# Six changes of order and of engine in a fused two-block fp32 transformer kernel on one core

## The reference

```python
def first_block(x, mem, ...):
    hn = rmsnorm(h, norm_mix_g)
    h = h + hybrid_mixer(hn, w_in, ...)          # gMLP, conformer conv, mLSTM, then @ w_out
    hn = rmsnorm(h, norm_x_g); mn = rmsnorm(mem, norm_mem_g)
    h = h + cross_attention(hn, mn, w_xq, w_xkv, w_xo)   # 4 heads of 256, 256 memory rows
    hn = rmsnorm(h, norm_ffn_g)
    h = h + conv_glu(hn, w_up, conv_f_w, conv_f_b, w_down)   # d_ff 2816
    return rmsnorm(h, final_g)

def second_block(x, mem, ...):
    z = rms_norm(h, g_mix_pre) @ w_in
    ya = swa_with_sinks(...)     # local attention, 8 heads of 64, window of 3 chunks of 64
    yh = hgrn2(...)              # gated linear recurrence
    y = concat([ya, yh]) @ w_out; h = h + rms_norm(y, g_mix_post)
    h = h + rms_norm(cross_attention_2(...), g_x_post)
    h = h + rms_norm((silu(u @ w_gate) * (u @ w_up)) @ w_down, g_ffn_post)
```

## Time and profile before

| | us |
|---|---|
| median of 3 runs | 2730.49 (2730.25 to 2730.56) |
| the profiled execution, its own time | 2729.75 |
| span of the profile | 2727.4 |
| PE busy | 2683.9 (98%) |
| DVE busy | 1768.8 (65%) |
| ACT busy | 1114.4 (41%) |
| POOL busy | 1307.8 (48%) |

### The profile page before, as it was taken

The page is one execution under the profiler, slowest core; times in us unless marked ns, Lnnn a source line. Parts: engine busy times, 40 slices in busy tenths (PEclk is TensorE's granted clock), DMA queues, the critical chain, the costliest instruction groups (busy, mean ns, idle before and its releaser), DMA issues.

```text
span 2727.4 us, 35252 instructions
## 1 busy us (share of the span) xinstructions
PE 2683.9 (98%) x12722; PEld 2196.3 (81%) x12722; DVE 1768.8 (65%) x2101; ACT 1114.4 (41%) x1854; POOL 1307.8 (48%) x766
## 2 busy tenths in 40 slices
PE   8999999999999999999999999999999999999999
PEld 6888787878778888888887778778887888888886
DVE  7888643345966666976845456784548655557775
ACT  4256622132433333444423524562446333334444
POOL 4313213545699999100466331454154888884002
PEclk9999999999999999999999999999999999999999
DMA  4101224342122222650422110332022433347413
GB/s 155 39 25 39 101 90 152 121 177 101 51 89 73 88 79 83 223 190 28 163 93 96 52 39 24 116 121 73 22 79 81 171 134 138 120 150 270 166 59 139
DMA packets 108712, 287.02 MB, mean 105 GB/s; under 512 B 9904, under 2 KB 20400, under 8 KB 107824
## 3 DMA queue, kind: packets, MB, share of 16 engines
q1 hardware_dynamic: 98336, 252.55, 26.4%
q10 hardware_dynamic: 10256, 32.86, 3.3%
HBM read 226.12 MB, written 59.24 MB: 105 GB/s over the span
## 4 chain that ended last, share of the span: by engine, by line
PE 89%; DVE 5%; ACT 2%; POOL 2%; issue 2%; DMA 0%; ACTq 0%; DVEq 0%; POOLq 0%; SPq 0%
PE products L993 22%; PE others L1515 14%; PE products L1515 13%; PE products L1088 8%; PE others L1598 7%; PE products L1598 7%; PE products L1426 2%; PE others L993 1%; PE products L1010 1%; PE products L1401 1%; PE others L1401 1%; PE products L1117 1%; PE products L1773 1%; PE others L1706 1%; PE others L1088 1%
## 5 line engine op out<-in xcount | busy, mean ns | idle before, releaser
L993 PE MATMUL products<-act_hi,w_hi 128*128 128x512 f32 x864 | 347.0, 402 | 1.4 <-DVE act_lo L2853 1.3
L993 PE MATMUL products<-act_hi,w_lo 128*128 128x512 f32 x864 | 336.9, 390 | 0.0
L993 PE MATMUL products<-act_lo,w_hi 128*128 128x512 f32 x864 | 336.9, 390 | 0.0
L871 POOL TENSOR_TENSOR w_lo<-w_raw,w_hi 128x512 fp32r<-128x512 f32 x200 | 309.7, 1557 | 37.6 <-ACT w_hi L2342 37.6
L786 POOL TENSOR_TENSOR w_hi<-w_raw,small 128x1024 fp32r<-128x1024 f32 x53 | 105.6, 1993 | 449.5 <-PE products L993 226.6
L993 PEld LDWEIGHTS products<-act_hi,w_hi 128*128 128x128 f32 x864 | 162.2, 188 | 41.7 <-issue 7.3
L2342 ACT ACTIVATE w_hi<-w_raw 128x512 fp32r<-128x512 f32 x240 | 146.2, 626 | 113.1 <-PE others L1515 50.1
L993 PEld LDWEIGHTS products<-act_hi,w_lo 128*128 128x128 f32 x864 | 162.2, 188 | 34.9
L993 PEld LDWEIGHTS products<-act_lo,w_hi 128*128 128x128 f32 x864 | 162.5, 188 | 30.8 <-issue 0.2
L904 POOL TENSOR_TENSOR w_lo<-w_raw,w_hi 128x512 fp32r<-128x512 f32 x8 | 10.4, 1294 | 363.7 <-ACT w_hi L2382 363.7
L793 POOL TENSOR_TENSOR w_lo<-w_raw,w_hi 128x512 fp32r<-128x512 f32 x64 | 99.2, 1571 | 136.5 <-ACT w_hi L2696 136.5
(11 more groups left out here) (638 smaller groups left out, 7377.7 us busy)
## 6 DMA issues: line engine op xcount, KB each, us to landing
w_raw<-wstream SPq DMA_DIRECT2D x147, 512.0 KB, 3.5
w_raw<-wstream SPq DMA_DIRECT2D x168, 256.0 KB, 2.6
work<-wstream SPq DMA_DIRECT2D x52, 512.0 KB, 4.4
parked_sums<-work SPq DMA_DIRECT2D x20, 1024.0 KB, 4.8
parked_hidden<-work SPq DMA_DIRECT2D x40, 512.0 KB, 2.9
raw<-parked_sums SPq DMA_DIRECT2D x28, 512.0 KB, 7.8
raw<-parked_hidden SPq DMA_DIRECT2D x20, 512.0 KB, 6.8
work<-parked_hidden SPq DMA_DIRECT2D x20, 512.0 KB, 7.7
```

Of the source, the lines that this page charges most:

```text
L871: pool.tensor_tensor(ring_lo[slot], part_source[(n - 1) % 7], ring_hi[slot].bitcast(F32), ALU.subtract)\
L993: last = pe.matmul(out[:, c], a[:, ws, w], x[:, k, c], start=(k == 0 and i == 0), stop=(k == KT - 1 and i == 2))
```

## The change

It moves and reassigns work; the arithmetic is the same up to which engine does it. (1) Block 19's high part is made by ACT and its low part by DVE, and ordered in the counts of y1_hi and y1_lo at position 7; POOL only counts it. The convolution's mean sums of tile 1 stand at part 5 instead of 4; the logs are spread between the head copies. (2) In the loop behind out1 DVE's key copy comes first, then the low weight part, then the sum and the low part of h; sums of the last tile are moved into the loop. (3) `weight_sums(3)` and `(4)` wait for chunks of the probabilities, and sums 7, 8, 9 stand behind splits q0+10, q0+11 and q0+12. (4) The root for ffn1 is made behind the third difference (k = 2). (5) Two squares are summed together in ffn2a. (6) In z2 PV of unit n - 5 stands right before the scores of n - 3 at k = 2, in the tiles n = 5 to 18; tile 19 does both of the last units.

```diff
+THIRD_AT = 7
@@ split_third, POOL
-                if b == 19:
-                    pool.wait_ge(s("product_quarters"), 4 * 17)
...
-            split_third(19, (s("y1_lo"), 8))
+            pool.wait_ge(s("y1_lo"), THIRD_AT + 1)
+            pool.sem_inc(s("weights_split"), 1)
+            made_elsewhere[0] += 1
@@ weight_sums, POOL
+                probs = {3: (3, 4), 4: (7, None)}.get(n, (None, None))
                 pool.wait_ge(s("block_moved"), 32 * (n + 1))
+                if probs[0]:
+                    pool.wait_ge(s("xa_probs"), XA0["1"] + probs[0])
                 pool.tensor_tensor(low_(1), low_(0), low_(1), ALU.add).then_inc(s("parts_summed"), 1)
                 pool.tensor_tensor(low_(0), up_(0), low_(0), ALU.subtract).then_inc(s("parts_summed"), 1)
+                if probs[1]:
+                    pool.wait_ge(s("xa_probs"), XA0["1"] + probs[1])
...
-                for n in {2: (0,), 4: (1,), 6: (2,), 9: range(3, 8), 10: (8,), 12: (9,)}.get(b - q0, ()):
+                for n in {2: (0,), 4: (1,), 6: (2,), 9: range(3, 7), 10: (7,), 11: (8,), 12: (9,)}.get(b - q0, ()):
@@ out1, PE
                     if i == 4:
                         last_back()
+                    if i == 5:
                         pe.wait_ge(s("ml_out"), NCH)
                         convolved_sums(1, "std_mean", lambda c: W[:, 3, c], s("cb_done"), 2)
...
-                    pe.wait_ge(s("y1_lo"), i + 1)
+                    pe.wait_ge(s("y1_lo"), i + 1 + (i >= THIRD_AT))
@@ ffn2a, PE
+                def squares_behind(k):
+
+                    if k and k % 2 == 0:
+                        square_of(k - 2)
+                        square_of(k - 1)
...
-                                  (lambda k: square_of(k - 1) if k else None) if (half, j) == (1, 0) else None)
+                                  squares_behind if (half, j) == (1, 0) else None)
                         if (half, j) == (1, 0):
-                            square_of(KT - 1)
+                            squares_behind(KT)
@@ z2, PE
+                        if k == 2 and n >= 5:
+                            window_values(n - 5)
                         if k == 2 and n < 19:
                             window_scores(n - 3)
                         if k == 4 and 4 <= n < 20:
                             window_turn(n - 4)
-                        if k == 6 and 4 <= n < 20:
+                        if k == 6 and n == 19:
                             window_values(n - 4)
@@ out1, ACT
+            def third_weight_high():
+
+                act.wait_ge(s("weights_loaded1"), 16 * 10)
+                act.wait_ge(s("product_quarters"), 4 * 17)
+                act.activation(w3_hi[:, 0, :], w_raw[:, 1, :], ACT.Copy).then_inc(s("y1_hi"), 1)
...
             head_high(6)
+            third_weight_high()
             convolved_squares(1)
             head_high(7)
+            convolved_logs(0)
             head_high(8)
+            convolved_logs(1)
+            head_high(9)
             convolved_roots()
-            head_high(9)
@@ ffn1, ACT
-            differences_high("ffn1")
-            roots("ffn1")
+            differences_high("ffn1", lambda k: roots("ffn1") if k == 2 else None)
@@ z2, ACT
+                if n > 4:
+                    window_out(n - 5)
                 turned_probs(n - 4)
                 if n < 19:
                     window_exponentials(n - 3)
-                window_out(n - 4)
+            window_out(15)
@@ out1, DVE
+            def third_weight_low():
+
+                dve.wait_ge(s("y1_hi"), THIRD_AT + 1)
+                dve.tensor_tensor(w3_lo[:, 0, :], w_raw[:, 1, :], w3_hi[:, 0, :].bitcast(F32), ALU.subtract).then_inc(s("y1_lo"), 1)
...
                 head_y(i)
+                if i == THIRD_AT:
+                    third_weight_low()
                 y1_low(i)
@@ behind out1, DVE
             for n in range(2, 2 * KT + 2):
-                if n < KT:
-                    weights_low("1", n)
-                if 2 <= n < 5:
+                if n < KT + 2:
+                    key("1", n - 2)
+                weights_low("1", n)
+                if n < 4:
+                    sums("q1", KT - 4 + n)
+                if n < 5:
                     split_low("q1", n - 2, h_tile, "x1")
-                if 2 <= n < KT + 2:
-                    key("1", n - 2)
-                if n >= KT:
-                    weights_low("1", n)
```

More of the change, by code:

```diff
@@ L2164, in convolved_squares, with convolved_logs @@
                 act.activation(W[:, n, :], W[:, 2 + n, :], ACT.Square, scale=0.125).then_inc(s("std_sq"), 1)
-            def convolved_roots():
[L2168 to L2172, removed]
+            def third_weight_high():
+                act.wait_ge(s("weights_loaded1"), 16 * 10)
+                act.wait_ge(s("product_quarters"), 4 * 17)
+                act.activation(w3_hi[:, 0, :], w_raw[:, 1, :], ACT.Copy).then_inc(s("y1_hi"), 1)
+            def convolved_logs(n):
+                act.wait_ge(s("std_var"), n + 1)
+                for h in range(2):
+                    last = act.activation(W[:, n, h * HALF:(h + 1) * HALF], std_slots[n][h], ACT.Ln, bias=epsc[:, 1:2])
+                last.then_inc(s("std_root"), 1)
+            def convolved_roots():
                 act.wait_ge(s("std_root"), 2)
@@ L2222, in _ @@
                 y1_high(10 + n)
-            act.wait_ge(s("y1_lo"), len(Y1_PARTS))
+            act.wait_ge(s("y1_lo"), len(Y1_PARTS) + 1)
             def memory(x):
@@ L3055, in y1_low @@
             def y1_low(i):
-                dve.wait_ge(s("y1_hi"), i + 1)
+                dve.wait_ge(s("y1_hi"), i + 1 + (i >= THIRD_AT))
                 dve.tensor_tensor(act_lo[:, Y1_PARTS[i][0], y1_tokens(i)], y1_source(i), hi_as_f32[:, Y1_PARTS[i][0], y1_tokens(i)],
                                   ALU.subtract).then_inc(s("y1_lo"), 1)
+            def third_weight_low():
+                dve.wait_ge(s("y1_hi"), THIRD_AT + 1)
+                dve.tensor_tensor(w3_lo[:, 0, :], w_raw[:, 1, :], w3_hi[:, 0, :].bitcast(F32), ALU.subtract).then_inc(s("y1_lo"), 1)
             def head_y(i):
@@ L3589, in residual, with to_tiles @@
                    .then_inc(s("h_made"), 1)
-            def to_tiles(name, norm, target, add, loaded=None, beside=None, each=None, early=None):
+            def to_tiles(name, norm, target, add, loaded=None, beside=None, each=None, early=None, sums_late=False):
                 for j in range(KT):
@@ L3610, in to_tiles @@
                         each(j)
-                    if j and not (early and j == KT - 1):
+                    if j and not ((early or sums_late) and j == KT - 1):
                         sums(norm, j - 1)
@@ L3615, in to_tiles @@
                         split_low(early, k, h_tile, early)
-                sums(norm, KT - 1)
+                if not sums_late:
+                    sums(norm, KT - 1)
             to_tiles("out1", "q1", h_tile, True, lambda j: (s(f"x_in{j}"), 32), lambda: memory("1"),
-                     lambda j: weights_low("1", j - 6) if j > 5 else None)
+                     lambda j: weights_low("1", j - 6) if j > 5 else None, sums_late=True)
             for n in range(2, 2 * KT + 2):
-                if n < KT:
-                    weights_low("1", n)
-                if 2 <= n < 5:
+                if n < KT + 2:
[4 more added lines that the diff above has]
+                if n < 5:
                     split_low("q1", n - 2, h_tile, "x1")
-                if 2 <= n < KT + 2:
-                    key("1", n - 2)
-                if n >= KT:
-                    weights_low("1", n)
                 if n == KT + 5:
```

## The result

The changed kernel is slower: a median of 2740.81 us (6 runs, 2740.49 to 2748.3) against 2730.37 for the kernel before (6 runs), ratio 1.0042 with a 95% interval of 1.0032 to 1.0052. The forecast was 2722.3 with a range of 2718.0 to 2727.0. So 18.5 us have to be explained, and the sign.

The account below looks back on a forecast made before the run. PE, busy 98% of the span, was taken as the bound. Terms 2.6 + 2.6 - 0.95 + 1.4 + 0.1 + 2.4 = 8.15 us won, from 2730.49 to 2722.3; range 2718.0 to 2727.0.

Parts of the forecast that it names:

- the 0.6 that was charged: Block 19: y1_low(7) comes late behind DVE's added subtraction, so PE is kept about 0.6 us at position 8.
- The gain (2.85): First cross attention: holding sums 3 and 4 removes PE's waits of 1.49 and 1.36 us behind the probabilities.
- Sum 9 can start 8.9 later plus 0.5: POOL before xo1: after sum 8 ends at 619.0, park, fetch and one load put sum 9's start at 628.4.
- The cycle of 14.1: POOL's weight sums: each takes 5.2 us and the next starts 8.9 later, after SP's parking and fetch.
- the 3.25 that I had kept for the range: split(q0+13): the longer w_lo time, if DVE interferes; PE then waits 3.0 instead of 2.1 us, 0.9 worse.
- The reason for taking 2.39: split(q0+13): DVE's work follows a PE block's end and w_lo starts long after one, so w_lo takes 2.39 us.
- ACT's squares are needed up to one product group later, never earlier: ffn2a: summing squares in pairs would not make PE wait for ACT; gain taken as 0.1 us.
- The sum of the excursions: z2: PV beside the scores saves PE 0.17 us in each of 14 tiles, 2.4 in all.
- ACT's window_out moves to the next tile, ahead of turned_probs; see the rival: z2: ACT copies PV's output one tile later; the risk was left to rival D, with no loss charged.
- rival D: z2: ACT copies PV's output too late for PE's turn, 1 us in 15 tiles costs 15: 2737.3; chance 0.04.
- Rivals A to C: Split(q0+13) in time 2718.5 (0.14); late, clock kept 2720.6 (0.18); key clock or PV gain fails 2724.0 to 2726.4 (0.21).
- The 0.04 for slower: Whole kernel: the chance given to a result slower than before by more than 5.46 us.

Follow-up runs that it names:

- z1: y4 with the merging of PV and scores undone, PV at k = 6 of its own tile again: 2718.81 us.
- y4: y2 with z2's probabilities behind the memory blocks' steps on DVE and ffn2a's squares summed one by one: 2715.92 us.
- x3: Changed kernel with DVE's scaling of a z2 tile moved ahead of the probabilities: 2726.83 us.
- y3: Changed kernel with POOL's splits for z2's tiles 12 and 13 waiting for DVE's probabilities of units 7 and 8: 2730.28 us.
- x4: Changed kernel with weight sum 8 behind split q0+12 and sum 9 behind split q0+13 on POOL: 2736.40 us.
- y1: x4 with SP's list mended too, loads of q0+12 and q0+13 ahead of the waits for sums 7 and 8: 2732.43 us.
- x2: Changed kernel with the held-back weight sums alone undone, no waits for probabilities and the old order of sums: 2736.08 us.
- x1: Changed kernel with the merging of PV and scores in z2 alone undone: 2728.25 us.
- y2: y1 and x3 in one, on the changed kernel: 2717.60 us.

## Why the prediction was wrong, point by point

**Part 1**, forecast 2.6: the trace shows 3.1. Right in kind. DVE made w3_lo in 1.22 and the addition beside it took 0.69, not 2.27; PE's wait at part 8 was 0.3 instead of the 0.6 that was charged.

**Part 2**, forecast 2.6: 2.9. The clock is 1.00 in k1 and two waits remain, but of 0.66 and 0.67, not 1.05 and 1.1 (changed kernel, timeline of PE):

```profile
386.25 0.38 PE L999 MATMUL products<-m_hi,w_hi 128*128 128x256 f32 x1 [0.66 <-POOLq L809]
...
390.06 0.38 PE L999 MATMUL products<-m_hi,w_hi 128*128 128x256 f32 x1 [0.67 <-POOLq L809]
```

v1 and q1 gave 0.6 of what k1 won back (0.2 to 0.8 in the other traces), and the 2.9 is what remained.

**Part 3**, forecast -0.95: measured 3.4 - 9.3 = -5.9 by the traces, and 2736.08 - 2740.81 = -4.7 between the medians. The gain (2.85) was rather more. The step that failed is the term "Sum 9 can start 8.9 later plus 0.5", with its place at 628.4. Sum 4 came where it was put: 557.4 less the 5.0 that the earlier parts had won is 552.4, and it started at 552.38. (The terms named there, 559.39 - 2.85 + 1.23, give 557.8; the difference decides nothing.) The cycle of 14.1 then did not hold where POOL meets DVE: 15.3 from sum 4 to 5, and 16.7 from sum 8 to 9, because sum 8's last two operations took 1.76 and 2.19 instead of 1.29 and the parking took 4.9 and the fetch 5.2 with q0+13's load among them. Sum 9 was 3.0 late against 628.4 - 5.0, and w_lo took 3.20 instead of 2.39, near the 3.25 that I had kept for the range. The reason for taking 2.39, that DVE would be quiet by then, failed: the sum and w_lo came so late that DVE's addition behind the end of a PE block (L2871, 1.46 at 633.06) was running when w_lo started at 633.52. PE was also 0.35 further ahead (8.2 instead of 5.0 + 2.85), and had already lost 1.3 at q0+12: 2.1 + 3.0 + 0.8 + 0.35 - 1.3 = 4.95, against 4.97 measured. The slow matmuls cost 2.9 instead of 1.7. The mechanism was right, and each of its terms was priced at its best. That q0+12 would be late by 1.06 was missed: the sum had left it 1.6 of slack, and its split ended at 620.6 instead of 618.3 (623.3 less 5.0).

**Part 4**, forecast 1.4: 2.5 by ffn1's start, of which 1.75 at the root and 0.8 in the ramp behind it.

**Part 5**, forecast 0.1 in the kernel's favour: 0.4 against it. "ACT's squares are needed up to one product group later, never earlier" looked at one side only: the buffer is also freed later.

**Part 6**, forecast +2.4: -11.7. The sum of the excursions was right (2.9 measured between z1 and y4). The step that failed is "ACT's window_out moves to the next tile, ahead of turned_probs; see the rival": I followed PV's consumers, ACT's window_out (rival D), and not what PE's earlier end of a tile meets, which is POOL's split being released and DVE's scaling behind the probabilities. That end moves by PV's own length in 14 tiles, and no line of the working had it. Rival D had the place and the piece of work right, ACT's four logs ahead of window_out in the tile of 1530, and there is one wait of 4.3 there, not 15 of 1 us; but x3 and y3 show that ACT was late because DVE was.

**The sum.** Forecast 8.15 won. Measured by the traces of single executions: 3.1 + 2.9 - 5.9 + 2.5 - 0.4 - 11.7 = -9.5 for the six parts. (The prediction's first paragraph counts five parts of one kind and two of the other; there are six, four and two.) The two traces have 1.2 in z1 and 0.6 in ffn2 on top, which belong to none of them (11.3 together); the medians differ by 10.4. Those 0.6 (+0.3 and +0.2 at single places of ffn2) stay open: they stand in y4 too and were not looked into.

The 0.04 for slower was the second fault. Rivals A to C were sizes of terms that the forecast had already; of the six parts only one, by rival D, had been asked what it could break elsewhere, and that one for a single consumer. The two parts that hold back or move what other engines wait for were the two that decided.

## What to carry to other kernels

When an operation is moved on the busiest engine, everything that this engine releases moves too: list what each following release starts (a split, a copy), and check the order in which it meets the other engines' work, because a shift of 1 us can turn who waits for whom. When work is held back on a queue, follow every queue that stands behind it until all have run out, and price a chain of many stages with its stretched durations, not with its undisturbed ones: here x4 only moved the wait from POOL's queue to SP's, and y1 removed it. Undo each part alone before judging the whole: four parts of this change were worth 8 us and two cost 18.

## What the runs showed of the hardware

The cost of a PE stall is not its length alone. Stalls of up to 1.58 were followed by no slow matmul in any trace, nor was the wait of 12.1 at the start (12 to 24 at 1.00). Behind one of 1.85 the granted clock fell both times it occurred (k1 before and xo1 in x3), and 1.7 was lost, (1 - granted clock) x 6. Behind all thirteen stalls of 3.0 to 5.9 it fell too, and the 12 us after each lost between 1.4 and 3.0, with no rule that I can see for which: a stall of 4.1 at the same place in z2 was followed by 1.7 in the changed kernel and by 2.7 in x2. The stall of 4.97 in xo1 cost 7.9 with the slow matmuls behind it.

The same pair of instructions on DVE and POOL cost nothing to PE in one order and 3.4 in the other, at two places. In the kernel before POOL's w_hi was stretched from 1.89 to 2.46 and nobody waited; 1 us earlier, DVE's probabilities took 3.25 for 1.22.

The spread of a kernel may tell of a race between engines. Of the kernels with 11 runs, those with a late split in xo1 (x1, x3, x4, y3) ranged over 5.5 to 11.5 us, and those without (x2, y1) over 2.4 and 3.4. In five runs each y4 and z1 ranged over 1.9 and 0.8, but y2, which has no late split either, over 3.8; so this is a hint and not a test.
